# Five seams of a hybrid attention and DeltaNet block are reordered

## The reference

```python
proj = x @ w_in                       # attention q/k/v, DeltaNet q/k/v, beta, decay, z, two gates
aq, ak = apply_rope(aq, cos, sin), apply_rope(ak, cos, sin)
y_attn = banded_sink_attention(aq, ak, av, attn_sink)       # chunks of 64, window of 128
dqkv = silu(causal_depthwise_conv(dqkv, conv_w))
o_dn = gated_delta_rule(l2n(dq), l2n(dk), dv, beta, g)      # scan over 16 chunks of 64
y_dn = rms_norm(o_dn) * dn_norm_w * silu(dz)
merged = gate_a * (y_attn @ w_branch_attn) + gate_b * (y_dn @ w_branch_dn)
x = layer_norm(ALPHA * x + merged @ w_out, ln1_g, ln1_b)
h = square(relu(x @ w_up))                                  # 4096 wide
x = layer_norm(ALPHA * x + h @ w_down, ln2_g, ln2_b)
```

## Time and profile before

| what | value |
|---|---|
| median of 3 executions | 1459.39 us (1458.61 to 1459.73) |
| the profiled execution, its own time | 1460.73 us |
| its span, first to last instruction | 1458.6 us |
| PE busy | 1424.6 us, 98% |
| DVE busy | 895.8 us, 61% |
| ACT, POOL busy | 525.5 and 316.9 us |
| mean granted clock of TensorE | 0.992 |

### The profile page before, as it was taken

The page is one execution under the profiler, slowest core; times in us unless marked ns, Lnnn a source line. Parts: engine busy times, 40 slices in busy tenths (PEclk is TensorE's granted clock), DMA queues, the critical chain, the costliest instruction groups (busy, mean ns, idle before and its releaser), DMA issues.

```text
span 1458.6 us, 22456 instructions
## 1 busy us (share of the span) xinstructions
PE 1424.6 (98%) x8570; PEld 1174.7 (81%) x8570; DVE 895.8 (61%) x1710; ACT 525.5 (36%) x1182; POOL 316.9 (22%) x341
## 2 busy tenths in 40 slices
PE   7999999999999999999998999999999999999996
PEld 7888887788888888778887888888888788888885
DVE  3655323565656656365617698666664677777778
ACT  3222212333323232252202435555554544444540
POOL 3666534142432424134820000000000000000000
PEclk9999999999999999999999999999999999999998
DMA  7222533423444233133541234333445866555422
GB/s 219 72 87 106 161 120 107 124 83 84 119 109 117 75 100 95 55 115 133 184 187 58 88 130 152 140 145 148 159 159 192 292 214 189 164 169 182 129 65 116
DMA packets 121007, 194.92 MB, mean 134 GB/s; under 512 B 27664, under 2 KB 67664, under 8 KB 118608
## 3 DMA queue, kind: packets, MB, share of 16 engines
q1 hardware_dynamic: 111984, 174.21, 36.6%
q10 hardware_dynamic: 8928, 19.40, 3.5%
HBM read 135.84 MB, written 57.74 MB: 133 GB/s over the span
## 4 chain that ended last, share of the span: by engine, by line
PE 91%; DVE 5%; ACT 1%; SPq 1%; DMA 1%; issue 1%; ACTq 0%; DVEq 0%
PE ps L1807 15%; PE ps L1742 10%; PE ps L1744 10%; PE ps L1743 10%; PE ps L2177 6%; PE ps L2178 6%; PE ps L2179 6%; PE ps L2160 5%; PE ps L2162 5%; PE ps L2161 5%; PE ps L1875 4%; PE ps L1815 2%; PE ps L1956 1%; PE ps L1907 1%; PE ps L1935 1%; PE ps L1946 1%
## 5 line engine op out<-in xcount | busy, mean ns | idle before, releaser
L713 POOL TENSOR_TENSOR ring2l<-raw,ring2h 128x256 fp32r<-128x256 f32 x180 | 176.6, 1012 | 3.6
L2177 PE MATMUL ps<-thi,shi 128*128 128x512 f32 x416 | 162.0, 390 | 0.0
L2179 PE MATMUL ps<-thi,slow 128*128 128x512 f32 x416 | 161.8, 389 | 0.0
L2178 PE MATMUL ps<-tlow,shi 128*128 128x512 f32 x416 | 161.8, 389 | 0.0
L1807 PE MATMUL ps<-xh,ring2h 128*128 128x512 f32 x304 | 122.5, 403 | 0.0
L1807 PE MATMUL ps<-xl,ring2h 128*128 128x512 f32 x304 | 122.3, 402 | 0.0
L1807 PE MATMUL ps<-xh,ring2l 128*128 128x512 f32 x304 | 119.7, 394 | 0.0
L710 POOL CAST ring2h<-raw 128x1024 fp32r<-128x1024 f32 x45 | 48.5, 1079 | 321.0 <-PE ps L1807 177.6
L1742 PE MATMUL ps<-xh,ring2h 128*128 128x512 f32 x288 | 112.2, 390 | 0.0
L1743 PE MATMUL ps<-xl,ring2h 128*128 128x512 f32 x288 | 112.0, 389 | 0.0
L1744 PE MATMUL ps<-xh,ring2l 128*128 128x512 f32 x288 | 112.0, 389 | 0.0
(11 more groups left out here) (348 smaller groups left out, 3236.3 us busy)
## 6 DMA issues: line engine op xcount, KB each, us to landing
raw<-in_wblk SPq DMA_DIRECT2D x55, 512.0 KB, 3.3
sraw<-hpark SPq DMA_DIRECT2D x104, 256.0 KB, 2.8
hpark<-hq SPq DMA_DIRECT2D x16, 1024.0 KB, 4.6
b<-in_wblk SPq DMA_DIRECT2D x64, 256.0 KB, 3.7
wraw<-in_wblk SPq DMA_DIRECT2D x30, 512.0 KB, 3.8
park<-ub ACTq DMA_DIRECT2D x50, 256.0 KB, 2.0
hpark<-hq SPq DMA_DIRECT2D x16, 768.0 KB, 5.0
park<-cout ACTq DMA_DIRECT2D x12, 512.0 KB, 2.6
```

What stands on the lines that cost most here:

```text
L713: ins = pool.tensor_tensor(lo[:, k:k + 2, :], src[:, k:k + 2, :], hi[:, k:k + 2, :].bitcast(F32), ALU.subtract)
L2177: mm(outp, shi[s][:, ts], thi[m][:, :], start=first, stop=False, skip_group_check=True)
L2178: mm(outp, shi[s][:, ts], tlow[m][:, :], start=False, stop=False, skip_group_check=True)
L2179: return mm(outp, slow[s][:, ts], thi[m][:, :], start=False, stop=final, skip_group_check=True)
```

## The change

Five places are changed; computation and results are the same.

1. **First loads.** The weights `wav` and tile 0 of x come in four quarters each (two blocks `k`), eight transfers, and PE waits for one quarter at a time; ACT's copy of tile 0 waits for all four. The semaphores `up_in` are used for them, so their later waits count 32 more. x lies in memory and in `xraw` tile by tile, so that a tile is 4 KB in a row for each partition.
2. **First recurrent tile.** The first step's list of fills is `[10, 8, 0, 8, 6, 6, 6, 6, 0, 6, 6, 6, 10, 10]` instead of `full`.
3. **Layer norm.** Output tile 5 comes ahead of the first two transposed tiles, tile 6 ahead of the next two, with ACT's and DVE's orders changed to match.
4. **Up to down.** ACT takes the third snapshot of the last pair before it splits anything for the down phase. SP issues `store_h(14)` behind the first eight down weights.
5. **Norms of four tiles inside the last pass.** The flush of pass 5 comes at steps 1 to 4 of pass 6 (before: 4 to 7), the statistics of tiles 0 to 3 a step behind each, their `deviation2` at step 6, `finish(0)` at step 7; only `finish(1)` to `finish(3)` are left behind the loop.

```diff
@@ sync
-            sp.dma_start(wavraw[:, :, :], A["wav"]).then_inc(wav_in, 16)
-            for t in range(NT):
-                sp.dma_start(xraw[:, :, t * P:(t + 1) * P], A["xT"][:, :, t * P:(t + 1) * P]).then_inc(x_in[t], 16)
+            for i in range(4):
+                ks = slice(2 * i, 2 * i + 2)
+                sp.dma_start(wavraw[:, ks, :], A["wav"][:, ks, :]).then_inc(up_in[i], 16)
+                sp.dma_start(xraw[:, 0, ks, :], A["xT"][:, 0, ks, :]).then_inc(up_in[i], 16)
+            for t in range(1, NT):
+                sp.dma_start(xraw[:, t, :, :], A["xT"][:, t, :, :]).then_inc(x_in[t], 16)
                 if t in (1, 3):
                     load_w(t // 2, t // 2)
...
-                if q < NP - 1:
+                if q < NP - 2:
                     store_h(q)
...
             for i in range(8):
                 load_down("B11", i, b11_in[0])
+            store_h(NP - 2)
             sp.wait_ge(sp_mm, last + U_P5)
@@ scalar
-                act.wait_ge(x_in[t], 16)
-                cp(xh[:, :, t * P:(t + 1) * P], xraw[:, :, t * P:(t + 1) * P]).then_inc(xh_ok, 1)
+                if t == 0:
+                    for i in range(4):
+                        act.wait_ge(up_in[i], 32)
+                else:
+                    act.wait_ge(x_in[t], 16)
+                cp(xh[:, :, t * P:(t + 1) * P], xraw[:, t, :, :]).then_inc(xh_ok, 1)
...
             for t in range(4):
                 norm(t)
-            for t in range(4):
-                x1_hi(t)
+            x1_hi(0)
+            x1_hi(1)
             norm(4)
             norm(5)
+            x1_hi(2)
+            x1_hi(3)
...
                     w_his(q + 1, 3, 7)
-                else:
-                    down_s(0)
-                    down_t(0)
                 snap(q, U_P1, 3, Q_S3)
                 if q == NP - 1:
-                    down_s(1)
-                    down_t(1)
+                    for n in range(2):
+                        down_s(n)
+                        down_t(n)
@@ vector
             combine(4)
+            combine(5)
             x1_lo(0)
             x1_lo(1)
             stats(4)
-            combine(5)
-            x1_lo(2)
-            x1_lo(3)
             stats(5)
             deviation(4, 6)
             place1(4)
             place1(5)
             combine(6)
-            stats(6)
+            x1_lo(2)
+            x1_lo(3)
             up_lo(0)
             up_lo(1)
+            stats(6)
             combine(7)
...
-                if j and 4 <= i < 8:
-                    flush(j - 1, i - 4)
+                f = i - (1 if j == 6 else 4)
+                if j and 0 <= f < 4:
+                    flush(j - 1, f)
+                if j == 6 and 0 < f <= 4:
+                    dve.wait_ge(fl_ok, 20 + f)
+                    half_stats(f - 1, 0)
+                if j == 6 and f == 5:
+                    deviation2(0, 4)
+                    dve.wait_ge(gb_in, 32)
+                if j == 6 and f > 5:
+                    finish(f - 6)
...
-            dve.wait_ge(fl_ok, 24)
-            for t in range(4):
-                half_stats(t, 0)
-            deviation2(0, 4)
-            dve.wait_ge(gb_in, 32)
-            for t in range(4):
+            for t in range(1, 4):
                 finish(t)
@@ tensor
-                if t == 0:
-                    pe.wait_ge(wav_in, 16)
-                pe.wait_ge(x_in[t], 16)
+                if t:
+                    pe.wait_ge(x_in[t], 16)
...
+                    if t == 0 and k % 2 == 0:
+                        pe.wait_ge(up_in[k // 2], 32)
...
-            step(None, 0, 1, 0, Fill([(19, 1), (20, 0)], lambda j: 1), full)
+            step(None, 0, 1, 0, Fill([(19, 1), (20, 0)], lambda j: 1), [10, 8, 0, 8, 6, 6, 6, 6, 0, 6, 6, 6, 10, 10])
...
             out_tile(4)
+            out_tile(5)
             x1_t(0)
             x1_t(1)
-            out_tile(5)
+            out_tile(6)
             x1_t(2)
             x1_t(3)
-            out_tile(6)
             out_tile(7)
```

More of the change, by code:

```diff
@@ L135, in hybrid_block @@
         xl = at("xl", 32, [P, KT, S], F32R)
-        xraw = at("xraw", 64, [P, KT, S])
+        xraw = at("xraw", 64, [P, NT, KT, P])
         y = at("y", 64, [P, 2 * NH, S])
@@ L321, in hybrid_block @@
         c_in = sem("c_in")
-        wav_in = sem("wav_in")
         av_mm = sem("av_mm")
@@ L1010, in up_split @@
                 else:
-                    act.wait_ge(up_in[n % 4], 16 * (n // 4 + (n % 4 > 1)))
+                    act.wait_ge(up_in[n % 4], 32 + 16 * (n // 4 + (n % 4 > 1)))
                     cp(slh[UP_SLOT[n % 4]][:, :, :], wraw[n % 4][:, :, :]).then_inc(up_hi, 1)
@@ L1077, in down_s @@
                     i = n - N_RUN
-                    act.wait_ge(x_in[i], 48)
+                    act.wait_ge(x_in[i], 48 if i else 32)
                     cp(shi[NSR + i][:, :], sraw[NSR + i][:, :]).then_inc(lsh_ok, 1)
@@ L1187, in _ @@
                 sl = slice(t * P, (t + 1) * P)
-                tt(xl[:, :, sl], xraw[:, :, sl], xh[:, :, sl].bitcast(F32), ALU.subtract).then_inc(xl_ok, 1)
+                tt(xl[:, :, sl], xraw[:, t, :, :], xh[:, :, sl].bitcast(F32), ALU.subtract).then_inc(xl_ok, 1)
             dve.wait_ge(c_in, 16 * 7)
@@ L1470, in combine @@
             def combine(t):
-                dve.wait_ge(x_in[t], 32)
+                dve.wait_ge(x_in[t], 32 if t else 16)
                 for n in range(2):
@@ L1581, in w_adds @@
                 for n in (2 * q, 2 * q + 1):
-                    dve.wait_ge(up_in[n % 4], 16 * (n // 4 + (n % 4 > 1)))
+                    dve.wait_ge(up_in[n % 4], 32 + 16 * (n // 4 + (n % 4 > 1)))
                 tt(w["S1"], w["S3"], w["A22"], ALU.add).then_inc(tx_sum, 1)
@@ L1752, in _ @@
                 for k in range(KT):
-                    last = mm(ps[4 + t % 2][:, 0:AVW], xraw[:, k, t * P:(t + 1) * P], wavraw[:, k, :], start=(k == 0), stop=(k == KT - 1))
+                    if t == 0 and k % 2 == 0:
+                        pe.wait_ge(up_in[k // 2], 32)
+                    last = mm(ps[4 + t % 2][:, 0:AVW], xraw[:, t, k, :], wavraw[:, k, :], start=(k == 0), stop=(k == KT - 1))
                 last.then_inc(av_mm, 1)
@@ L2229 @@
     arrays = {
-        "x": x2, "xT": x2.T.reshape(KT, P, S).transpose(1, 0, 2), "wblk": wblk,
+        "x": x2, "xT": x2.T.reshape(KT, P, NT, P).transpose(1, 2, 0, 3), "wblk": wblk,
         "wav": np.concatenate([col["av"], col["beta"], col["da"]], 1).reshape(KT, P, AVW).transpose(1, 0, 2),
```

## The result

| | before | after |
|---|---|---|
| median (lowest to highest) | 1459.56 us of 4 (1458.61 to 1460.22) | 1448.17 us of 4 (1446.65 to 1448.88) |
| ratio, 95% interval | | 0.9921 (0.9904 to 0.9938) |
| profiled execution, its span | 1460.73, 1458.6 | 1448.78, 1446.7 |
| mean granted clock | 0.992 | 0.996 |

A forecast was written before the change was run, and what follows sets the result against it. The prediction took PE as the bound, busy 1424.6 of 1458.6 us. Its terms 3.4 + 1.3 + 7.1 + 0.9 + 1.2 = 13.9 us, taken from the median of 1459.4, gave 1445.5, range 1441 to 1450.5.

The forecast's parts named there:

- seam 1: First loads: PE starts on the first quarter, the stage ends at 21.3 instead of 24.75; gain 3.4 us (1.5 to 4.4).
- 7 tiles of 1.9: First loads: after tile 0 is done at 7.5, seven tiles of 1.9 us give 20.8, plus 0.5 for late tiles.
- The prediction's own sign of being wrong: First loads: the prediction is wrong if PE waits for tiles 1 to 4 of x by more than 1.5 in all.
- The rival "the start gives nothing": First loads: all 16 engines are full from 2 us, so an early start only moves PE's wait; 1449, chance 0.08.
- Seam 2: First recurrent tile: fills moved among small products remove 2.1 us of waits, more long-short changes cost 0.8; gain 1.3 (0 to 2.1).
- Seam 3: Layer norm: PE's waits of 4.1 us go and the clock no longer falls, 3.05 more; gain 7.1 (lower bound 4.1).
- Seam 4: Up to down: third down step arrives 3.9 us earlier, less 3.0 for the clock; gain 0.9 (0.5 to 3.9).
- The new gap of 2.4 us: Before the third down step: PE waits 2.4 us for the third pair's split, behind DVE's chain of 10.7 us.
- it falls again and costs 3.0: Behind the new gap before the third down step: the granted clock falls again, costing 3.0 us.
- Seam 5: Norms in the last pass: DVE is 0.3 us late at PE's first late tile instead of 1.5; gain 1.2 (0.3 to 1.5).
- the slower rival: Last pass, steps 97 to 103: it becomes DVE's, PE has repeated gaps and the clock stays low; 1467, chance 0.02.
- The rival of the held clock: Before the third down step: the clock holds through the new gap, 3.0 us more gained; 1442.5, chance 0.27.

The follow-up runs named there:

- the whole version: Kernel after the change with only the quarters undone: `wav` in one transfer, tile 0 of x in one, new layout of x kept; 1445.41 us.
- both squares: Stores or weights first, against ACT splits or snapshot first; snapshot to last matmul 327.1, 324.5, 327.8, 325.0 us; without the clock's part 324.4, 322.8, 326.2, 323.3.

## Why the prediction was right or wrong

The total lies inside the range, but partly by luck: seam 1 came out 4.3 below its term and under its lower bound of 1.5, and the other four gave back 2.4, part of it by the scatter of the clock at seams 3 and 4.

**Seam 1, the step that failed: "the stage ends at 21.3, a gain of 3.4".** Its first half was right: quarters issued at 1.20 to 4.03, PE's start at 3.35 (said: 3.5). "The quarters land 0.9 apart, so tile 0 is done at 7.5": it was done at 8.49, since the quarters landed 0.9 to 1.7 apart and PE took 1.1 instead of 1.0 for each. And "7 tiles of 1.9" was wrong in two ways. Tile 1 landed at 10.0, because SP issued it 2.8 later than in the whole version (4.50 against 1.70) and the small pieces ran at 263 GB/s against 371. And PE, with waits at 4.62 and 8.49, stayed at the lower clock until 14.8; I had charged the low clock to tile 0 alone. Of the two, the clock is the larger: 3.06 us against 1.84 of waits, by the sum above. The prediction's own sign of being wrong, waits for tiles 1 to 4 of more than 1.5 in all, came true with 1.61. The rate of the earlier trace rows was applied to the whole stage, though the quarters are small transfers with 1 KB in a row: the layout that earned the rate was cut up by the split. Over six profiles with the new first loads the start lies between 23.91 and 26.57, mean 25.2; the old loads gave 24.50 and 25.09, whole tiles in the new layout 23.48 and 22.78. So the split costs 2.1 and the layout gives 1.7; the two edits of one seam nearly cancelled. Tile 7, on which I spent most care, was never late.

The rival "the start gives nothing", 1449 with a chance of 0.08, is what happened at this seam. Its reason, full engines and a wait that only moves, was right for 1.84 of the 4.04 us; the clock's 3.06 was in no rival, and the bytes did not come as fast as before but slower. That the total is near its 1449 is chance, since the other seams gave 2.4 more than it reckoned with. The Trainium skill, Perfetto Trace Analysis, "DMA Optimizations", names both halves: splitting may finish the task sooner if the DMA engines are generally idle, and small DMAs (below 2 KB) have a significant overhead each. The traces agree with the first: with whole transfers the engines were busy for 0.97 and 0.98 of the time from 2.1 to 7.7 us, and the split lost. With the second they agree in direction only, 263 GB/s with runs of 1 KB against 371 with 4 KB, since the number of issues changed with them. I had cited the first and weighed it too low.

**Seam 2: 1.3 forecast, 1.5 measured**, again 1.55 when taken back. Only the 0.62 stayed, as said; by difference, what the four more changes between long and short matmuls cost was 0.6 (2.1 less 1.5) instead of 0.8; no run varied them alone.

**Seam 3: 7.1 forecast, 7.8 measured.** Both waits went, nothing came late, clock 1.00: the mechanism is as said, and taking it back returned 4.07 of waits. Of the 0.7 above the forecast no row tells more; it is open. What the experiment adds is that the clock's part is not fixed: 6.8 us at 0.50 in the profile before, 3.4 when the same gaps came back. By medians the seam is worth 6.0, so that 7.8 is what it gave against a profile with a long stretch at 0.50.

**Seam 4: 0.9 forecast, 2.1 measured.** The new gap of 2.4 us was there, at its place, with 2.63 and its cause, DVE's chain (10.7 said, 10.6 measured); the arrival at the third step moved by 3.6 (said: 3.9). The term that was mis-sized is the clock: "it falls again and costs 3.0". It fell and cost 1.6, being at 0.50 for 3.4 instead of 6.8 us. The credit for the snapshot's order was wrong: "the snapshot comes first ... and the last product follows without a gap" is true and worth nothing, as both squares show; the store order alone gives 2.6, or 1.6 with the clock taken out. With the clock taken out of both kernels the seam gave 1.0, and the forecast's 3.9, less the 2.7 that it counts for the clock before, is 1.2: the path was right, and the surplus over 0.9 is the clock's.

**Seam 5: 1.2 forecast, 1.5 measured.** DVE was at its first late flush at once instead of 0.3 late; PE never waited for a split in the last pass, so the slower rival had nothing to stand on.

**The rival of the held clock** (0.27) was no rival but a scatter. Of the ten kernels with the new gap, the profile shows the clock fallen in seven (behind gaps of 2.08 to 3.17 us) and held in three (gaps of 2.45, 2.40 and 2.63 us). The whole version held behind the very gap of the kernel after:

```profile
1132.32 0.47 PE L2182 MATMUL ps<-thi,shi 128*128 128x512 f32 x1 [2.63 <-DVE tlow L1636]
```

```profile
1132.30:1140.00 7.70, 7.68 (x34) 6.36 (x35) 3.49 (x6) 0.06 (x1) 0.00 (x0) 1.00 0.73 253
```

Its fourth stretch is 323.4 against 325.0, so the fall costs 1.6; the other two that held have 323.2. My argument from the gap's length ("2.4 is nearer to the 2.78") decided between two things that both happen: the clock fell behind 2.08 and held behind 2.63.

Sum: seam 1 was 4.3 too high, the others together 2.4 too low; the profiled execution after lies 0.6 above its median, the one before 1.2.

## What to carry to other kernels

Before a first load is split to start the matmul engine sooner, ask what the pieces do to the transfers behind them: eight issues put the next tile 2.8 us later in the queue, and the rate was 263 GB/s instead of 371 while PE waited for bytes. The start of an engine is no gain if it then waits between tiles, above all where its clock is still low: of 4.04 us won here, 1.84 went to waits and 3.06 to work at the lower level; starting 2.4 us later and running through was 1.9 us faster. Before two stretches are compared, take out what the clock did in each: half of a gain of 2.1 was its scatter here. And where two waits hang on one chain, undo each half alone before crediting it: here the early loads were the gain and the reorder beside them moved the wait.

## What the runs showed of the hardware

- After the same gap of 2.63 us TensorE's granted clock fell to 0.50 in one profile and stayed at 1.00 in another; after the same two gaps (2.78 or 2.77, and 1.30 us) it was at 0.50 for 6.8 us once and for 3.4 once. A gap's length did not decide it: it fell behind one of 2.08 us. With identical first loads it rose at times from 8.6 to 16.4 us. One fall costs 1.6 us; that this makes up most of the 2 us by which executions of one kernel differ is likely, but not shown, since each kernel has one profile. The Trainium skill, TensorE: Matmul & The Clock Gate, Part 1, says that the number of matmuls at the lower level at the start of a kernel varies between runs of the same kernel. The traces agree as far as two kernels with the same first loads show it: whole in the new layout, PE started at 5.73 and 5.75, and the clock rose at 11.7 and 10.3.
- 20 matmul records on zeros, issued while nothing else could run, had the clock up at 5.1 to 6.3 us instead of 10.3 to 11.7 in the same kernels without them.
